# Moving the modulation product into the input projection, and adding every second gathered row on VectorE

## What is computed

```python
# first block, mixer: a wide input product
hn = rmsnorm(h, g_mix); z = hn @ w_in            # then MLA attention, retention, gates, merge

# first block, PEER feed-forward: 8 heads x 16 picks = 128 expert rows for each token
eidx = (e1 * PEER_NKEYS + e2).reshape(T, 128)    # from two top-16 lists of each head
gates = softmax(sc)
act = gelu(einsum('td,tkd->tk', xt, peer_u[it])) # a dot with one gathered row each
y   = einsum('tk,tkd->td', gt * act, peer_v[it]) # a weighted sum of 128 gathered rows
h   = h + y

# second block: the modulation, which depends on c and weights alone
mod = silu(c) @ w_ada + b_ada                    # 6 x 1024 values, from 25 MB of weights
```

## Time and profile before

| what | value |
|---|---|
| median of 3 runs | 3019.58 us |
| the profiled execution | 3025.01 us (span from first to last instruction 3023.3 us) |
| `p1` | 29.6 to 304 us |
| `peer_gather` | 789 to 2266 us, 49% of the span |
| first and last `fetch_u` | 847.3 and 2226.5 us |
| PE / DVE / ACT / POOL busy over the span | 80% / 52% / 23% / 39% |

### The profile page before, as it was taken

One profiled execution on the slowest core, in us unless ns is written; L12 is line 12 of the kernel. 1 busy time (PEld: TensorE's weight loads), 2 busy tenths in 40 slices (PEclk: granted clock), 3 DMA queues, 4 the chain that ended last, 5 costly groups with the idle time before them and its releaser, 6 DMA issues. The chain is left out here.

```text
span 3023.3 us, 24883 instructions
## 1 busy us (share of the span) xinstructions
PE 2414.3 (80%) x7902; PEld 1475.0 (49%) x7902; DVE 1575.5 (52%) x3274; ACT 696.2 (23%) x1482; POOL 1182.1 (39%) x1144
## 2 busy tenths in 40 slices
PE   6999897898427678776787777777888978699988
PEld 6778464476413233232232333333336844588877
DVE  4322435544677755676556765555534435545534
ACT  3123005513101111111111111111113334333322
POOL 1000204001067777777777777777751100100000
PEclk8999557998758888888898888888888968899999
DMA  3332100022079999999999999999973200222222
GB/s 115 80 91 64 65 1 17 20 80 100 14 279 388 371 414 418 399 384 371 409 420 400 386 391 419 420 419 415 417 310 101 67 33 22 75 100 97 83 69 97
DMA packets 204655, 666.86 MB, mean 221 GB/s; under 512 B 24528, under 2 KB 39648, under 8 KB 201456
## 3 DMA queue, kind: packets, MB, share of 16 engines
q0 software_dynamic: 147456, 536.94, 44.7%
q1 hardware_dynamic: 57088, 128.57, 13.1%
HBM read 663.32 MB, written 2.10 MB: 220 GB/s over the span
## 5 line engine op out<-in xcount | busy, mean ns | idle before, releaser
L1535 PE MATMUL gather_Y<-gather_v,gather_diag 128*128 128x512 f32 x2048 | 1031.7, 668 | 432.5 <-ACT gather_diag L1504 432.5
L1535 PEld LDWEIGHTS gather_Y<-gather_v,gather_diag 128*128 128x128 f32 x2048 | 435.2, 216 | 1027.1 <-issue 542.7
L1455 DVE CUSTOM_DVE_ANT_0 gather_junk<-gather_u,peer_xtok 128x1024 f32<-128x1024 f32 x512 | 626.9, 1226 | 533.7 <-DMA gather_u<-in_peer_u,gather_eidx 501.5
L1434 POOL DMA_INDIRECT gather_u<-in_peer_u,gather_eidx x512 | 523.4, 1022 | 262.4 <-issue 155.8
L1439 POOL DMA_INDIRECT gather_v<-in_peer_v,gather_eidx x512 | 546.9, 1068 | 179.1 <-issue 132.3
L1504 ACT ACTIVATE gather_diag<-all_ident,gather_a 128x128 f32<-128x128 f32 x512 | 184.0, 394 | 470.2 <-PE gather_Y L1535 470.0
L1509 ACT ACTIVATE gather_gel<-gather_dots 128x8 f32<-128x8 f32 x64 | 13.3, 208 | 754.6 <-DVE gather_dots L1455 754.6
L492 DVE TENSOR_TENSOR p_cut<-m1h_raw,p_cut 128x512 fp32r<-128x512 f32 (+2 forms) x96 | 63.1, 660 | 187.0 <-ACT p_cut L516 187.0
L1891 PE MATMUL ffn_acc<-m2f_hs,ffn_cut 128*128 128x512 f32 x352 | 137.8, 392 | 9.7 <-DVE ffn_cut L1939 9.7
L577 PE MATMUL o_acc<-o_wcut,o_acut 128*128 128x512 f32 x304 | 121.1, 398 | 21.8 <-DVE o_wcut L610 21.8
L1892 PE MATMUL ffn_acc<-m2f_hs,ffn_cut 128*128 128x512 f32 x352 | 137.6, 391 | 0.0
(11 more groups left out here) (337 smaller groups left out, 3648.3 us busy)
## 6 DMA issues: line engine op xcount, KB each, us to landing
gather_ada<-in_w_ada SPq DMA_DIRECT2D x48, 512.0 KB, 6.5
m2f_raw<-in_w_up SPq DMA_DIRECT2D x22, 1024.0 KB, 4.8
m1h_raw<-in_w_in SPq DMA_DIRECT2D x80, 256.0 KB, 2.7
m2h_raw<-in_w_in SPq DMA_DIRECT2D x48, 256.0 KB, 2.7
m_down_ring<-in_w_down SPq DMA_DIRECT2D x22, 512.0 KB, 3.5
gather_u<-in_peer_u,gather_eidx POOLq DMA_INDIRECT x512, 7.6
gather_v<-in_peer_v,gather_eidx POOLq DMA_INDIRECT x512, 7.6
m_merge_ring<-in_w_ret_out SPq DMA_DIRECT2D x8, 512.0 KB, 4.6
```

Of the source, the lines that this page charges most:

```text
L1434: pool.indirect_dma_start(u[:, n % RU, :], None, u_dram, bass.IndirectOffsetOnAxis(col(eidx, n), 0)).then_inc(u_landed[n % RU], 16)
L1455: dve.tensor_tensor_reduce(junk[:, n % 2, :], u[:, n % RU, :], xtok[:, n // PICKS, :], 1.0, 0.0, ALU.mult, ALU.add, col(dots, n)).then_inc ...
L1535: ins = pe.matmul(Y[:, t % 2, h, :], diag[:, n % RD, :], v[:, n % RV, h * BANK:(h + 1) * BANK], start=(k == 0), stop=(k == PICKS - 1))
```

## The change

1. The modulation leaves `peer_gather` and becomes a guest of `p1`: class `Modulation`. SP loads the 48 rows of `w_ada` between the raw loads of `p1`, VectorE makes one row's product after the split of a unit, in 4 units of 5, so in units 0 to 59 of 96. Its buffers lie in the gate tile `zaT`, which ScalarE first writes when job 8 is copied out (`yields=8`, a wait before that).
2. In `peer_gather` only even picks go through ScalarE's diag and TensorE. Odd picks are "folded" on VectorE: resid += v row x weight, one instruction over 1024 elements, placed after the dot of the pick 16 later. `fetch_v(n)` waits, for odd n, on the fold of n - 8.
3. The stages without a hardware loop no longer use a Block, but a `Straight`: each engine's program is emitted in line, followed by a barrier of the five engines.

```diff
+class Straight:
+    def __exit__(self, *a):
+        self.nc.multi_engine_barrier(self.ENGINES)
+    def vector(self, program):
+        program(self.nc.vector)
...
+class Modulation:
+    BANKS, SLOTS, EVERY = 0, 2, 5
...
+    def rows_at(self, u):
+        first = lambda n: min(self.rows, n - n // self.EVERY)
+        return range(first(u), first(u + 1))
+
+    def load(self, sp, j):
+        if j >= self.SLOTS:
+            sp.wait_ge(self.summed, j - self.SLOTS + 1)
+        sp.dma_start(self.ada[j % self.SLOTS], self.w_ada[j * P:(j + 1) * P, :]).then_inc(self.landed[j % self.SLOTS], 16)
+
+    def sync(self, sp, u):
+        if u == KD:
+            for j in range(self.SLOTS):
+                self.load(sp, j)
+        for j in self.rows_at(u - KD):
+            if j + self.SLOTS < self.rows:
+                self.load(sp, j + self.SLOTS)
...
+    def vector(self, dve, u):
+        for j in self.rows_at(u):
+            if j == 0:
+                dve.wait_ge(self.active, 1)
+            dve.wait_ge(self.landed[j % self.SLOTS], 16 * (j // self.SLOTS + 1))
+            if j >= 1:
+                dve.wait_ge(self.summed, j)
+            dve.tensor_tensor_reduce(self.junk, self.ada[j % self.SLOTS], self.cond, 1.0, 0.0, ALU.mult, ALU.add, self.mod[:, j:j + 1]).then_inc(self.summed, 1)
...
@@ def project
                 sp.dma_start(raw[:, u % RAW, 0:wd.shape[1]], wd[k * P:(k + 1) * P, :]).then_inc(landed[u % RAW], 16)
+                guest.sync(sp, u)
...
             def copy_out(i):
                 out = jobs[i][1]
+                if i == yields:
+                    guest.finish(act)
...
@@ def peer_gather
+        on_pe = lambda n: n % 2 == 0
+        consumed = lambda n: (used, n // 2 + 1) if on_pe(n) else (folded, n // 2 + 1)
-        block = ph.block()
-
-        @block.sync
-        def _(sp):
-            for j in range(ADA):
-                if j >= 2:
-                    sp.wait_ge(summed, j - 1)
-                sp.dma_start(ada[:, j % 2, :], w_ada[j * P:(j + 1) * P, :]).then_inc(ada_landed[j % 2], 16)
+        block = ph.straight()
...
             def fetch_v(n):
                 if n >= RV:
-                    pool.wait_ge(used, n - RV + 1)
+                    pool.wait_ge(*consumed(n - RV))
...
+            def fold(n):
+                dve.wait_ge(v_landed[n % RV], 16 * (n // RV + 1))
+                dve.wait_ge(weighed, n // B + 1)
+                if n > 1:
+                    dve.wait_ge(folded, n // 2)
+                y = resid[:, n // PICKS, :]
+                dve.scalar_tensor_tensor(y, v[:, n % RV, :], col(a, n), y, ALU.mult, ALU.add).then_inc(folded, 1)
...
-                if n % EVERY == EVERY - 1 and n // EVERY < ADA:
-                    condition(n // EVERY)
+                if n >= LAG + 4 and not on_pe(n - LAG - 4):
+                    fold(n - LAG - 4)
                 if t >= 1 and k == LAG + 24:
                     collect(t - 1)
             weigh(N // B - 1)
-            dve.wait_ge(summed, ADA)
-            dve.tensor_tensor(mod[:], mod[:], b_ada[:], ALU.add)
+            for n in range(N - LAG - 4, N):
+                if not on_pe(n):
+                    fold(n)
             collect(NT - 1)
...
                     for n in range((b - 1) * B, b * B):
-                        spread(n)
+                        if on_pe(n):
+                            spread(n)
...
             for n in range(N):
-                accumulate(n)
+                if on_pe(n):
+                    accumulate(n)
```

More of the change, by code:

```diff
@@ L106, in __call__, with __init__, __enter__, tensor @@
         self.engine.wait_ge(self.sem, self.n)
+class Straight:
+    ENGINES = (mybir.EngineType.PE, mybir.EngineType.Activation, mybir.EngineType.DVE, mybir.EngineType.SP, mybir.EngineType.Pool)
+    def __init__(self, nc):
+        self.nc = nc
+    def __enter__(self):
+        return self
+    def __exit__(self, *a):
+        self.nc.multi_engine_barrier(self.ENGINES)
+    def tensor(self, program):
+        program(self.nc.tensor)
+    def vector(self, program):
+        program(self.nc.vector)
+    def scalar(self, program):
+        program(self.nc.scalar)
+    def sync(self, program):
+        program(self.nc.sync)
+    def gpsimd(self, program):
+        program(self.nc.gpsimd)
 class Phase:
@@ L142, in block, with straight @@
         return self.stack.enter_context(self.nc.Block())
+    def straight(self):
+        return self.stack.enter_context(Straight(self.nc))
 def bc(ap, axis, n):
@@ L383, in tensor, with __init__, sync, scalar @@
             ins.then_inc(self.turned, 1)
+class Modulation:
+    BANKS, SLOTS, EVERY = 0, 2, 5
+    def __init__(self, ph, space, b_ada, mod, w_ada):
+        self.ada = [space[:, 2 * r:2 * r + 2, :].rearrange("p a n -> p (a n)") for r in range(self.SLOTS)]
+        self.cond, self.junk = (space[:, a:a + 2, :].rearrange("p a n -> p (a n)") for a in (4, 6))
+        self.b_ada, self.mod, self.w_ada = b_ada, mod, w_ada
+        self.rows = 6 * KD
+        self.landed = [ph.sem(f"ada_landed{r}") for r in range(self.SLOTS)]
+        self.active, self.summed = ph.sem("cond_active"), ph.sem("mod_summed")
+    def rows_at(self, u):
[5 more added lines that the diff above has]
+        sp.dma_start(self.ada[j % self.SLOTS], self.w_ada[j * P:(j + 1) * P, :]).then_inc(self.landed[j % self.SLOTS], 16)
+    def sync(self, sp, u):
+        if u == KD:
[4 more added lines that the diff above has]
+                self.load(sp, j + self.SLOTS)
+    def scalar(self, act, u, T):
+        if u == 0:
+            act.activation(self.cond, self.cond, ACT.Silu).then_inc(self.active, 1)
+    def finish(self, act):
+        act.wait_ge(self.summed, self.rows)
+    def vector(self, dve, u):
[6 more added lines that the diff above has]
+            dve.tensor_tensor_reduce(self.junk, self.ada[j % self.SLOTS], self.cond, 1.0, 0.0, ALU.mult, ALU.add, self.mod[:, j:j + 1]).then_inc(self.summed, 1)
+            if j == self.rows - 1:
+                dve.wait_ge(self.summed, self.rows)
+                dve.tensor_tensor(self.mod[:], self.mod[:], self.b_ada[:], ALU.add)
+    def gpsimd(self, pool):
+        pass
+    def tensor(self, pe, u, T):
+        pass
 def project_loads(jobs):
@@ L403, in project @@
         cut = ph.sb("cut", [P, CUT, 2, BANK], F32R)
-        NB = 6 if guest is not None else 8
+        NB = 8 - guest.BANKS
         acc = ph.ps("acc", [P, 8, BANK])
@@ L1405, in peer_gather @@
         diag = ph.sb("diag", [P, RD, P])
-        ada = ph.sb("ada", [P, 2, D])
         S = ph.ps("S", [P, 4, BANK])
         Y = ph.ps("Y", [P, 2, 2, BANK])
-        keys, iota, cond, b_ada = (tables[n] for n in ("keys", "iota", "cond", "b_ada"))
+        keys, iota = tables["keys"], tables["iota"]
         top = TopK(ph, S, iota, eidx, gates)
@@ L1495, in _ @@
         def _(act):
-            act.activation(cond[:], cond[:], ACT.Silu).then_inc(c_active, 1)
             top.exponent(act, 0)
@@ L2026, in program @@
             s = ph2.sem("consts")
[L2027 removed]
+            block = ph2.straight()
             @block.sync
```

91 lines of the change are left out of this document (41 added, 50 removed).

## The result

The changed kernel takes 3101.77 us, the median of 5 runs (3098.46 to 3128.23). The kernel before, run beside it, takes 3020.97 (3015.65 to 3026.82, 5 runs). The ratio is 1.0291, with a 95% interval of 1.0269 to 1.0312 (the two medians alone stand at 1.0267): the change makes the kernel 2.7 to 2.9% slower. The profiled execution of the changed kernel took 3128.23 us, so it is 26 above its median, and its span of 3126.4 is 103 us longer than the span before, where the medians differ by 81.

The account below looks back on a forecast made before the run. GpSimd's unbroken chain of fetches in `peer_gather` was taken as the bound, with the DMA limit beside it at 2.50 us a pick. Terms -6 + 22 + 20 - 12 + 5 - 2 = +27 gave 3046 us, range 2988 to 3115.

Parts of the forecast that it names:

- (b): Gather picks with `TopK`, ahead of the dense part, tiles 0 to 2: folds add +22 us; ends -6 and +50.
- (a): Gather picks without `TopK`: less DMA traffic against fetches hit by dots and folds, -6 us; ends -36 and +92.
- (c): Dense part of `TopK`, three tiles: GpSimd's new wait of `fetch_v` for a fold, +20 us; ends +10 and +30.
- (d): End of the gather: last picks shared by PE and DVE folds, -12 us; ends -14 and -8.
- (e): Modulation's products and loads in `p1`: mainly an unhidden start, +5 us; ends +2 and +18.
- fourth rival: In `p1`, the modulation's products don't hide, loads at 6.5 us: +18 instead of +5, 3060 us; chance 0.05.
- (f): Straight instead of Block at some 15 stage borders: -2 us; ends 0 and -5.
- DMA is the bound and the folds fit: Rival for the gather: bytes limit it, folds fit: -34 us in all, 2986 us; chance 0.27.
- Folds are hit as in the `TopK` stretch everywhere: Rival for the whole gather: no full DMA queue spaces landings, +143 us, 3163 us; chance 0.13.
- The new wait is nothing: Rival for the dense part: GpSimd's lead rarely exceeds 4 picks, about +0 in all, 3020 us; chance 0.12.

Follow-up runs that it names:

- e4: Changed kernel with each fold replaced by a one-operand sum over the v row, odd picks' weighted sum left out: 3054.40 us, ratio 1.0113.
- e2: Changed kernel without folds: modulation in `p1`, all 512 picks through ScalarE's diag and TensorE: 3017.66 us, ratio 0.9997.
- e1: Kernel before with only Straight instead of Block in stages without a hardware loop: 3019.26 us, ratio 0.9996.
- e5: e2 with each dot replaced by a one-operand sum over the u row, product with the token left out: 2967.20 us, ratio 0.9813.
- e8: e2 with e7's slower rows and the token copied to PSUM as the dot's operand, `Y` single-buffered: 2957.76 us, ratio 0.9779.
- e7: Changed kernel with the modulation's rows in `p1` begun at unit 4, 5 rows in 7 units: 3092.65 us, ratio 1.0227.
- e6: Changed kernel with 12 slots of v instead of 8, `fetch_v(n)` waiting for the fold of n - 12: 3086.45 us, ratio 1.0201.
- e11: Changed kernel, all folds kept, with the token in PSUM and `collect` at pick LAG + 4: 3018.23 us, ratio 0.9997.
- e10: e1 with the token in PSUM for the dots, the modulation left in the gather: 2989.37 us, ratio 0.9896.

## Why the prediction was wrong in size

The direction and the bound were right, and 3101.8 lies within the range of 2988 to 3115; but the forecast was 3046, and the time lies outside the forecast's own range of 3015 to 3080. A forecast of +0.9% met +2.7% over the 3019.58 on record. Step by step:

(b) *Picks with `TopK`: this is the step that failed*, by the term that it priced at +22 (ends -6 and +50) and that measured +61. By the other profiles it is +50 to +70. The mechanism was right, as e4 shows: take the second operand away and more than half of the folds' cost here goes. What was off is the price of a fold. I took the mean price of a two-operand instruction in the loose stretch, 0.30 us, from rows in which DVE had 52 us of 170 free, as if a further instruction cost what the existing ones cost. It costs 77.5 / 87 = 0.89 us in this profile (0.56 with its second operand, mostly for its own hits, and 0.33 for pushing the dots into other positions), and 0.64 in the lowest pair of profiles. The upper end of +50 was only as high as the lowest of these sums. The forecast fetch of 1150 ns is 1273. My statement that DVE's fullness raises the hits was a bound of +50 only; it should have been the centre. The gain from the modulation's absence is not what failed: it is 7.0 us by e2 against e1, for the 5.6 of the working, and both within the scatter of single profiles.

(a) *Picks without `TopK`: -6 forecast, +18 measured* (+21.0 in tiles 0 to 2, -2.9 in tile 3). The floor of 2.50 that the step built on is not there any more: without the modulation the gathers reach 409 GB/s, 2.56 us a pick (e5, e8), and the 328.1 us of tile 3 are within 2 of e8's 326.1. The forecast fetch of 960 to 990 ns for tile 3 is 982, and 2.58 a pick stands where 2.60 was forecast. But the phase that settles in tile 3 doesn't settle everywhere: picks 96 to 127 take 80.0 us in tile 2 and 85.8 in tiles 0 and 1, at 1.08 us a fetch. e2, without folds, has the same in tile 1 (87.2), and e7 in tile 1 alone (87.1, tile 0 at 79.2). The folds are not what is met there: of the fetches after pick 76 of tiles 0 to 2, all 152 that last over 0.96 us end 0.81 after a dot and none after a fold. So a tile can come out of `TopK` in a good or a bad pattern, and what decides it is open. It may be why the runs of one kernel lie up to 30 us apart, but with one profile of each kernel that is not shown. The closing sentence of the prediction had named a settled phase as a danger; the step priced it only in its upper end.

(c) *The dense part: +20 forecast, +18.6 measured.* The wait is where the working had put it: at v 57 and v 59 of tiles 0, 1 and 2, six times, 17.6 us in all (the other two of the list are in the end). Tile 1 in the timeline of POOL:

```profile
1457.80 1.68 POOL L1526 DMA_INDIRECT gather_v<-in_peer_v,gather_eidx  x1 [0.78 <-DVE all_resid L1554]
...
1466.84 1.67 POOL L1526 DMA_INDIRECT gather_v<-in_peer_v,gather_eidx  x1 [3.63 <-DVE all_resid L1554]
```

The working had 6.8 us a tile; it is 6.6 in tiles 0 and 2 and 4.4 in tile 1. What it left out is on the same lines: a fetch that a fold lets go runs into DVE's next instruction and lasts 1.68 us. What it left out on the other side is that part of the waiting takes the place of hits, since a POOL that stands can't be hit: e6 takes the wait away and gets back 10.5 of the 18.6. The two nearly cancel, and that the total of 18.6 came so close to 20 is in part luck.

(d) *The end: -12 forecast, -8.9 measured.* From the start of the last dot (2345.03 in the changed kernel) to the end of the last fold it is 22.9 us, where the forecast had 18.6, and PE's last stretch is 20.7 us for the forecast 16. The timeline of POOL there:

```profile
2342.62 1.88 POOL L1526 DMA_INDIRECT gather_v<-in_peer_v,gather_eidx  x1 [0.67 <-DVE all_resid L1554]
...
2347.73 1.96 POOL L1526 DMA_INDIRECT gather_v<-in_peer_v,gather_eidx  x1 [1.98 <-DVE all_resid L1554]
2350.90 1.62 POOL L1526 DMA_INDIRECT gather_v<-in_peer_v,gather_eidx  x1 [1.22 <-PE gather_Y L1624]
```

Three of these last fetches are let go by a fold or by PE and run into a DVE instruction of two operands, so that they last 0.94 + 1.02 + 0.68 = 2.6 us more than the 0.94 that the step had for each.

(e) *`p1`: +5 forecast, +13.5 measured*, near the +18 of the fourth rival but by another way. The load lands after 4.4 us, not 3.5 as assumed nor 6.5 as the rival feared; with one product and the reuse of a slot, the first rows came at a pace of 3.0 to 3.4 us (not 2.4), above the 2.6 allowed, and the start was 4.3 us. e7 asks for 2.9 and begins later, and gets 9.9 of the 13.5 back.

(f) *Straight: -2 forecast, -0.2 to -1.0 at the border of `p1`* and nothing measurable in total (e1).

Of the rivals, *DMA is the bound and the folds fit* fell with e2: with the 25 MB gone and no folds, the gather gained 8 us by the profiles and some 15 by the medians, not 36. *Folds are hit as in the `TopK` stretch everywhere* was to hold if fetches outside it lasted over 1.05 us; tile 3 says 0.98, two stretches of tiles 0 and 1 say 1.08. In these two stretches the fetches were as long as it says, but by the dots and not by the folds, as e2 has them without any fold. *The new wait is nothing* fell with the list of waits.

The Trainium skill ("SBUF — State Buffer", Who interferes with whom) says that a DVE instruction with at most one SBUF input does not contend with GpSimd, its two-port modes aside. With that rule the traces of e5 and e8 agree, with 0.95 to 0.96 us a fetch in the mean. Its inference that descriptor generation is spared is contradicted by 1.95 against 0.94 at the same position.

## What to carry to other kernels

When one engine's chain of equal short instructions is the bound and the traces show another engine lengthening them, an instruction added to that other engine must be priced at the margin (here 0.64 to 0.89 us for 1.28 us of "free" DVE time), not at the mean (0.30) of those already there. Look first at where the operands lie: moving the operand that all 512 dots share into PSUM gave 84 us in the changed kernel (e11) and 30 in the kernel before (e10) without a change of any DVE time, and only with it was it worth 32 us to take the modulation out of the stage. A load that is moved under a stage with a full engine is better paced by its landing time over its slots, with its first use later than its first landing: the two together gave 9.9 us back in e7.
